# Router logits of a two-layer transformer block: x stationary against padded router columns stationary in four column groups

## The reference, cut to what matters

```python
def hier_moe(h, gw, gb, ew, eb, w_gu, w_down):
    tok = h.reshape(-1, D)                                   # 512 tokens in layer 0, 256 in layer 1
    g_logits = (tok @ gw + gb)                               # gw: 1024 x 4
    e_logits = (tok @ ew + eb).reshape(-1, 4, 4)             # ew: 1024 x 16
    ...                                                      # top group, its top 2 experts, weights
    for e in range(16):
        gu = tok @ w_gu[e]
        act = silu(gu[:, :512]) * gu[:, 512:]
        y = y + combine[:, e:e + 1] * (act @ w_down[e])
```

## Time and profile before

| | |
|---|---|
| timed executions, us | 1131.35, 1131.76, 1138.03; median 1131.76 |
| profiled execution | span 1129.0 us (its page gives no other time) |
| busy | PE 946.4 us, PEld 593.7, VectorE 390.2, ScalarE 281.2, GpSimd 187.3 |
| mean granted TensorE clock | 0.934 of full |
| DMA | 313.53 MB, mean 278 GB/s |
| the changed line, L817 | 96 matmuls of 128x20, 96 weight loads |

### The profile page before, as it was taken

One profiled execution on the slowest core, in us unless ns is written; L12 is line 12 of the kernel. 1 busy time (PEld: TensorE's weight loads), 2 busy tenths in 40 slices (PEclk: granted clock), 3 DMA queues, 4 the chain that ended last, 5 costly groups with the idle time before them and its releaser, 6 DMA issues. The chain is left out here.

```text
span 1129.0 us, 24486 instructions
## 1 busy us (share of the span) xinstructions
PE 946.4 (84%) x9652; PEld 593.7 (53%) x9653; DVE 390.2 (35%) x1003; ACT 281.2 (25%) x756; POOL 187.3 (17%) x284
## 2 busy tenths in 40 slices
PE   3899989899999599989986169997898688798675
PEld 2354635556555367656663057674664455455343
DVE  2100026667434412111110373627653622222123
ACT  4121144456333011111110261125643100000001
POOL 0030013300021343333431431004001100000001
PEclk9999999999999699999997679998999699999798
DMA  9973315565243879999999696532313979999991
GB/s 376 363 240 144 149 75 224 206 215 216 76 167 149 345 304 404 421 424 424 424 425 420 238 383 227 224 110 114 113 75 142 396 316 424 426 426 412 429 403 57
DMA packets 54662, 313.53 MB, mean 278 GB/s; under 512 B 12202, under 2 KB 17444, under 8 KB 36020
## 3 DMA queue, kind: packets, MB, share of 16 engines
q1 hardware_dynamic: 33664, 279.19, 60.9%
q0 software_dynamic: 10192, 27.88, 7.2%
q10 hardware_dynamic: 10724, 5.29, 1.6%
HBM read 303.88 MB, written 14.75 MB: 282 GB/s over the span
## 5 line engine op out<-in xcount | busy, mean ns | idle before, releaser
L556 PE MATMUL psum<-hT,weights 128*128 128x512 f32 (+1 forms) x336 | 123.2, 527 | 4.7 <-ACT lat L1196 3.2
L1007 PE MATMUL psum<-weights,lat 128*32 128x256 f32 x1568 | 95.9, 397 | 20.4 <-DMA weights<-in_exp_w_gu_dram 8.7
L556 PEld LDWEIGHTS psum<-hT,weights 128*128 128x128 f32 x336 | 66.0, 198 | 58.5 <-issue 48.3
L921 PE MATMUL psum<-weights,lat 128*32 128x256 f32 x992 | 70.0, 441 | 27.3 <-issue 16.2
L1007 PEld LDWEIGHTS psum<-weights,lat 128*32 128x32 f32 x1568 | 61.5, 114 | 51.2 <-issue 29.0
L1669 DVE TENSOR_REDUCE st<-psum 128x1 f32<-128x512 f32 (+1 forms) x96 | 56.7, 599 | 47.3 <-PE psum L672 20.9
L1826 DVE STREAM_TRANSPOSE lat<-lat 128x256 f32<-128x256 f32 x41 | 18.2, 445 | 151.7 <-PE psum L1007 143.1
L921 PEld LDWEIGHTS psum<-weights,lat 128*32 128x32 f32 x992 | 38.6, 124 | 56.4 <-issue 43.1
L1289 ACT ACTIVATE R<-psum,st 128x512 f32<-128x512 f32 (+1 forms) x78 | 48.2, 618 | 78.8 <-DVE st L1669 46.9
L788 PE MATMUL psum<-weights,hT 128*128 128x512 f32 x144 | 63.5, 595 | 0.0
L1020 PE MATMUL psum<-weights,lat 128*32 128x256 f32 x832 | 51.2, 379 | 1.7 <-issue 0.9
(11 more groups left out here) (342 smaller groups left out, 1572.1 us busy)
## 6 DMA issues: line engine op xcount, KB each, us to landing
weights<-in_exp_w_gu_dram SPq DMA_DIRECT2D x42, 2048.0 KB
weights<-in_ada_w_dram SPq DMA_DIRECT2D x24, 2048.0 KB, 8.5
weights<-in_exp_w_down_dram SPq DMA_DIRECT2D x22, 2048.0 KB
hT<-in_exp_w_gu_dram SPq DMA_DIRECT2D x10, 2048.0 KB
R<-in_exp_w_gu_dram SPq DMA_DIRECT2D x10, 2048.0 KB
spare_w<-in_exp_w_down_dram SPq DMA_DIRECT2D x10, 2048.0 KB
weights<-in_w_in_dram SPq DMA_DIRECT2D x6, 2048.0 KB, 13.9
weights<-in_w_out_dram SPq DMA_DIRECT2D x4, 2048.0 KB, 9.4
```

Of the source, the lines that this page charges most:

```text
L556: mm = nc.tensor.matmul(t[:, lo:hi], w[:, k, col:col + P], hT[:, k, lo:hi], start=(k == 0), stop=(k == KD - 1))
L921: mm = nc.tensor.matmul(gu_ps[BLK * j:BLK * j + BLK, 0:256], xgT[:, k, :], w[:, k % 4, j, :, :], start=(k == 0), stop=(k == KD - 1), skip_ ...
L1007: mm = nc.tensor.matmul(gu_ps[BLK * j:BLK * j + BLK, 0:256], xgT[:, k, :], w[:, k % 4, j, :, :], start=(k == 0), stop=(k == KD - 1), skip_ ...
```

## The change

The product for the logits is turned round. Before, a tile of x (128x128) was the weight and 20 router columns were moved through, eight times, and the sum was made in PSUM over all eight. After, the router's columns, padded from 20 to 32, are the weight, and 128 tokens are moved. The eight products go in turn to the four 32-column groups of the array, so that PSUM holds four partial sums of the transposed logits, each 32x128, one above the other. ScalarE copies them to SBUF (`parts_out`), and one product with these parts as the weight and four stacked identities moving adds the four and turns them, to 128x20 in the same bank. The last product of a tile is put one iteration later, ahead of `turn_out`. GpSimd sets the padding to zero; the constants grow by 20 columns.

```diff
+    put("four_parts", np.tile(np.eye(32)[:, 0:20], (4, 1)))
...
-        w_rta = part(extra, 3200, 2 * KD * 20, "p (a k c) -> p a k c", a=2, k=KD)
+        w_rta = part(extra, 3200, 2 * KD * 32, "p (a k c) -> p a k c", a=2, k=KD)
...
+        lg_parts = [part(lat, 4 * 256 + i * P, P) for i in range(2)]
...
-            def logits(L, tt):
+            def logit_parts(L, tt):
                 t = take("lg", L, tt, banks=spare())
                 for k in range(KD):
                     if k % 4 == 0:
                         pe.wait_ge(*at("xT", L, tt, k // 4))
-                    mm = nc.tensor.matmul(t[:, 0:20], hT[:, k, tt * P:(tt + 1) * P], w_rta[:, tt // 2, k, :], start=(k == 0), stop=(k == KD - 1))
-                mm.then_inc(*mark(f"pe_out{L}", ("filled", "lg", L, tt)))
+                    g = k % 4
+                    mm = nc.tensor.matmul(t[32 * g:32 * g + 32, 0:P], w_rta[:, tt // 2, k, :], hT[:, k, tt * P:(tt + 1) * P],
+                                          start=(k < 4), stop=(k >= 4), skip_group_check=True)
+                mm.then_inc(*mark(f"pe_out{L}", ("filled", "lg_parts", L, tt)))
+
+            def logits(L, tt):
+                pe.wait_ge(*at("lg_parts", L, tt))
+                nc.tensor.matmul(psum[:, M.bank_of["lg", L, tt], P:P + 20], lg_parts[tt % 2], C("four_parts"), start=True, stop=True)\
+                    .then_inc(*mark(f"pe_out{L}", ("filled", "lg", L, tt)))
...
+                    if tt > 1:
+                        logits(L, tt - 2)
                     turn_out(L, tt - 1)
                     out_diff(L, tt)
-                    logits(L, tt - 1)
+                    logit_parts(L, tt - 1)
+                logits(L, n - 2)
                 turn_out(L, n - 1)
+                logit_parts(L, n - 1)
                 logits(L, n - 1)
...
+                def parts_out(tt):
+                    act.wait_ge(*at("filled", "lg_parts", L, tt))
+                    act.wait_ge(*at("dsum", L, n - 1))
+                    a(lg_parts[tt % 2], psum[:, M.bank("lg", L, tt), 0:P], ACT.Copy).then_inc(*mark(S, ("lg_parts", L, tt)))
...
                     half_stats(S, ("o", L, tt), 13, tt, out_half(tt))
+                    if tt:
+                        parts_out(tt - 1)
...
                         half_stats(S, ("x2", L, tt), 32, tt, x_half(tt), lambda: evict(n - 1))
+                        parts_out(n - 1)
...
-                    stt(dst, read(v, "lg", L, tt)[:, 0:20]...
+                    stt(dst, read(v, "lg", L, tt)[:, P:P + 20]...
...
+                nc.gpsimd.memset(w_rta[:, :, :, 20:32], 0.0)
                 for s in range(2):
-                    gt(w_rta[:, s, :, :], w_rt[:, :, :], amp[L][:, 2, :, s]...
+                    gt(w_rta[:, s, :, 0:20], w_rt[:, :, :], amp[L][:, 2, :, s]...
```

More of the change, by code:

```diff
@@ L225, in hybrid_block @@
         w_pool = part(extra, 2944, 2 * P, "p (j n) -> p j n", j=2)
-        w_rta = part(extra, 3200, 2 * KD * 20, "p (a k c) -> p a k c", a=2, k=KD)
-        w_rt = part(extra, 3520, KD * 20, "p (k c) -> p k c", k=KD)
-        row_sb = part(extra, 3680, P)
+        w_rta = part(extra, 3200, 2 * KD * 32, "p (a k c) -> p a k c", a=2, k=KD)
+        w_rt = part(extra, 3712, KD * 20, "p (k c) -> p k c", k=KD)
+        row_sb = part(extra, 3872, P)
         w_extra = extra[:, :].rearrange("p (k c j f) -> p k j c f", k=4, c=2, j=QUADS)
@@ L1791, in logits @@
                     dst = lg[:, 0:20 * n].rearrange("p (g t j) -> p g t j", g=5, t=n)[:, :, tt, :]
-                    stt(dst, read(v, "lg", L, tt)[:, 0:20].rearrange("p (g j) -> p g j", g=5), rs[:, 36, tt:tt + 1],
+                    stt(dst, read(v, "lg", L, tt)[:, P:P + 20].rearrange("p (g j) -> p g j", g=5), rs[:, 36, tt:tt + 1],
                         rt_c[:, tt // 2, :].rearrange("p (g j) -> p g j", g=5), ALU.mult, ALU.add)\
@@ L2203, in vectors @@
                     g_.wait_ge(*at("filled", "lg", L - 1, tiles(L - 1) - 1))
+                nc.gpsimd.memset(w_rta[:, :, :, 20:32], 0.0)
                 for s in range(2):
-                    gt(w_rta[:, s, :, :], w_rt[:, :, :], amp[L][:, 2, :, s].unsqueeze(2).to_broadcast([P, KD, 20]), ALU.mult)
+                    gt(w_rta[:, s, :, 0:20], w_rt[:, :, :], amp[L][:, 2, :, s].unsqueeze(2).to_broadcast([P, KD, 20]), ALU.mult)
                     ins = gt(w_rtb[:, :, s, :], w_rt[:, :, :], mod[L][:, 24:32, s].unsqueeze(2).to_broadcast([P, KD, 20]), ALU.mult)
```

## The result

The changed kernel takes 1160.69 us (median of 4 runs, 1155.28 to 1162.54), the kernel before, run beside it, 1134.89 us (4 runs, 1131.35 to 1138.61): ratio 1.0227, 95% interval 1.0199 to 1.0256. The profiled execution has a span of 1160.5 us.

The account below looks back on a forecast made before the run. Experts' weight streams bound by memory, the stage ahead by TensorE. Two tiles, each 1.71 us removed, 0.72 and 0.22 added, give 1.54, taken as 1.5: 1131.76 - 1.5 = 1130.3 us, range 1127.6 to 1133.0.

Parts of the forecast that it names:

- Sum on the path: Two tiles' logits ahead of the expert weight streams: 2 x (1.71 - 0.72 - 0.22) = 1.54 us saved, taken as 1.5.
- Result: Whole kernel: both weight streams and everything behind start 1.5 us earlier, median 1131.76 - 1.5 = 1130.3 us.
- Removed: Old logits on TensorE, 1.71 us a tile; only two of six tiles lie on the path: -3.42 us.
- the parts: New 16 instructions of 32-column weights in four groups on TensorE: 0.66 to 0.79 us a tile, taken as 0.72.
- the closing product: Float32 product on TensorE adding and turning the four partial sums, ahead of `turn_out`: 0.22 us a tile.
- rival 1: TensorE's new products: weight loads don't overlap, 107 ns each, a tile 0.41 us longer; +0.8 us, 1132.6; chance 0.04.
- Moved to other engines, at nothing: ScalarE's 0.28 us copy a tile, VectorE's later read of the logits and GpSimd's memset cost the path 0 us.
- The tails: Last tiles of both layers: neither gains; layer 0's 0.45 us VectorE wait goes, but ranking still ends with GpSimd's addition.
- rival 2: First expert blocks: TensorE's full clock returns later, one block more cold loses 2.27 us; +0.8 us, 1132.6; chance 0.12.
- Rival 4: Ahead of the last turn: the spare 0.55 us is missing, each tail 0.95 us later, 1132.2; chance 0.05.
- Rival 3: Weight stream: its order of transfers, gathers and stores takes back the 1.5 us gain, 1131.8; chance 0.16.

Follow-up runs that it names:

- before_24: Kernel before plus 24 empty semaphore increments on TensorE ahead of layer 1's routing, products unchanged: 1162.78 us, ratio 1.0253.
- after_skip227: Changed kernel plus 227 jumped-over and 5 testing instructions on TensorE, layer 1's expert loop one 256-instruction block behind its old place: 1129.13 us, ratio 0.9966.
- layer0_only: Changed kernel with the old logits kept in layer 1, jumped-over instructions putting layer 1's expert loop where the kernel before has it: 1130.88 us, ratio 0.9972.

## Why the prediction was wrong

**Sum on the path, and Result** ("the start of both weight streams and everything behind them moves by the same 1.5 us"). This is the step that failed. The added instructions were priced only by their execution, where they stand. That 24 more of them move everything behind in TensorE's program was no term of the sum, and it is worth +29 us here (before_24, ratio 1.0253), nearly twenty times the sum: layer 1's loop over the experts is then fetched anew in each pass, and TensorE stands 15 us at each of its two jumps back. No rival held it. It could have been asked from what lay there before: 60 instruction packets, the waits for "issue" in the loop's first pass, and a loop 6.36 blocks long. With the rule that the later runs fit, an eighth block at 92 of 256 places, that is an estimate of one chance in three for a large loss; neither the rule nor the size of the loss stood in the profile of before.

**Removed, the parts, the closing product.** Right. The parts took 345.22 - 344.65 = 0.57 us from start to start, and the run of `out_diff` ahead of them 3.53 us for 3.43 before, the 0.10 of entering: 0.67 (forecast 0.72, ends 0.66 and 0.79). The product took 0.14 (0.22). For two tiles 2 x (1.71 - 0.67 - 0.14) = 1.80; the stage got 1.68 shorter, and the forecast was 1.54.

**The Trainium skill's rule on weight loads** (rival 1; page TensorE: Matmul & The Clock Gate, Part 3, The mechanism). Not so here: 16 of this form in 0.57 us, though all four column groups use every row.

**Moved to other engines, at nothing.** Held: ScalarE's copy takes 0.26 to 0.28 us, and each closing product inside the tiles starts without a wait. VectorE does wait for two of them, 4.63 and 4.41 us; it waited some 6 us for the turned tile there before, and the stage is none the longer for it.

**The tails.** As forecast in layer 0. VectorE reads the last logits without waiting for TensorE, and the ranking still loses the time beside GpSimd (timeline of the changed kernel):

```profile
367.35 0.62 PE L827 MATMUL psum<-cst,lat 128*128 128x20 f32 x2 [0.40 <-ACT lat L1377]
368.36 0.23 DVE L1814 SCALAR_TENSOR_TENSOR lg<-psum,rs,rt_c 128x20 f32<-128x20 f32 x1
368.52 2.36 POOL L2264 TENSOR_TENSOR spare_w<-R,spare_w 128x1024 f32<-128x1024 f32 x1 [13.55 <-DVE R L1807]
368.62 2.35 DVE L1823 TENSOR_TENSOR picked<-lg 128x80 f32<-128x80 f32 x1
```

The ranking's first step ends at 370.97 us, 10.62 after expert 1's load; GpSimd's addition, which the prediction took for its end, was 368.81 - 358.11 = 10.70 behind it in the kernel before.

**The other rivals.** The clock (rival 2): the first block of layer 0 is cold in both, 5.3 to 6.3 us in the changed profiles, 5.5 to 6.6 in the others; no block more. In layer 1 the second block of the experts runs cold in some profiles of either form (5.35 us in after_skip227, whose layer 1 has the new form, and in layer0_only, whose layer 1 has the old; 3.66 before), so that doesn't come from the form; behind the two pauses the changed kernel does have cold blocks more, as a consequence of them. Rival 4: the first turn comes 1.62 us after ScalarE's statistics as before (363.18 - 361.56), so its spare time was there. Rival 3, the gain swallowed: not seen at the old place.

**The size of the gain at the old place** is not settled. The stage gives 1.68 us, and layer 0's last load comes 1.7 us earlier on the mean of the eight profiles with the new form than of the eight others (278.9 against 280.6 us after that first load). Timed, it is 3.8 us (2.2 to 5.7) in after_skip227, 3.2 (1.4 to 4.9) in layer0_only. No step of the traces accounts for more than 1.7, which the second interval allows and the first doesn't.

## What to carry to other kernels

An edit on an engine whose program is longer than what it keeps also moves every loop behind it: count the instructions that an edit adds, and ask of each later loop how many blocks of 256 it can touch. The count alone didn't show on which side of an edge the loop lies; here only runs with the loop moved did. Where a small edit gives a large loss in a stretch that it doesn't touch, look first at the instruction queue's packets and at "issue" in the chain, then pad by instructions that are jumped over until the loop lies where it did; only then is the edit itself measured. Here that turned 1.0227 into 0.9966.

## What the runs showed that I had not expected

- Twenty-four empty instructions on TensorE made a kernel of 1133 us take 1163; twelve made no difference that shows, and a whole block of 256 none.
- A jump back to a loop that is fetched anew cost 15 us each time under a full weight stream, and 11 to 12 with a quarter of the loads, where the DMA engines were idle through the pause's second half; one to a loop that is held 1.9.
- Removing the loop costs too: straight code beside a full weight stream had pauses of 3.3 to 7.0 us.
- Matmuls with 32-column weights in four column groups, 128 columns moved, ran 16 in 0.57 us, 36 ns each, and 0.10 us more in the run ahead of them for entering.
